# Two transformer blocks in one fp32 kernel: w_v loaded earlier into places of its own, and GpSimd, ScalarE, VectorE and TensorE work before v and k put in another order

## The reference

```python
def first_block(x, p, ...):
    h = rms_norm(x, pre_norm_gain[i])
    q, k, v, z_a, b_gate, c_gate, u, z_c = jnp.split(h @ w_in[i], N_IN_PARTS, axis=-1)
    ...
    mixed = jnp.concatenate([attn, conv_out], axis=-1) @ w_out[i]
    x = x + rms_norm(mixed, post_norm_gain[i])
    e = rms_norm(p[i] @ w_ple_proj[i], ple_norm_gain[i])
    x = x + jax.nn.sigmoid(x @ w_ple_gate[i]) * e

def gmlp_mixer(h, w_in, ln_g, ln_b, w_s, b_s, w_out):
    u, v, z = jnp.split(h @ w_in, 3, axis=-1)
    ...
    y = u * s * jax.nn.silu(z)
    return y @ w_out

def second_block(x, ...):
    y = gmlp_mixer(rms_norm_2(h, a_pre_g[i]), a_w_in[i], ..., a_w_out[i])
    h = h + rms_norm_2(y, a_post_g[i])
    kv_in = rms_norm_2(h, kv_norm_g)
    k_shared = (kv_in @ w_k).reshape(...)
    v_shared = (kv_in @ w_v).reshape(...)
    ...
    y = swa_mixer(rms_norm_2(h, b_pre_g[j]), k_shared, v_shared, b_w_in[j], b_sinks[j], b_w_out[j])
    h = h + rms_norm_2(y, b_post_g[j])
```

## Time and profile before

| what | value |
|---|---|
| median of 3 runs | 882.74 us (882.06 to 883.52) |
| the profiled execution | 882.54 us, its span 880.8 us |
| granted TensorE clock | 0.999 |
| TensorE busy | 863.5 us, 98% of the span |
| VectorE, ScalarE, GpSimd busy | 576.5, 383.7, 514.8 us |
| bytes moved by DMA | 106.84 MB |

### The profile page before, as it was taken

One profiled execution on the slowest core, in us unless ns is written; L12 is line 12 of the kernel. 1 busy time (PEld: TensorE's weight loads), 2 busy tenths in 40 slices (PEclk: granted clock), 3 DMA queues, 4 the chain that ended last, 5 costly groups with the idle time before them and its releaser, 6 DMA issues.

```text
span 880.8 us, 11945 instructions
## 1 busy us (share of the span) xinstructions
PE 863.5 (98%) x4196; PEld 718.3 (82%) x4196; DVE 576.5 (65%) x918; ACT 383.7 (44%) x828; POOL 514.8 (58%) x568
## 2 busy tenths in 40 slices
PE   8999999999998999999999999999997999999997
PEld 6888888888887788888888888888887888888875
DVE  6125648875998489676766625556995457788624
ACT  4123333433664377555112311113775446667622
POOL 7766555691249822318975048772369797566352
PEclk9999999999999999999999999999999999999999
DMA  7533222453952468994732253526951222112202
GB/s 198 165 122 97 72 78 67 142 122 73 238 194 71 138 148 176 221 234 147 175 118 85 89 169 107 133 80 163 213 173 66 72 75 93 49 48 73 72 1 95
DMA packets 83691, 106.84 MB, mean 121 GB/s; under 512 B 11953, under 2 KB 54449, under 8 KB 83634
## 3 DMA queue, kind: packets, MB, share of 16 engines
q1 hardware_dynamic: 72752, 85.12, 30.3%
q0 software_dynamic: 10880, 20.97, 14.1%
q10 hardware_dynamic: 2, 0.00, 0.0%
HBM read 103.98 MB, written 2.10 MB: 120 GB/s over the span
## 4 chain that ended last, share of the span: by engine, by line
PE 90%; POOL 5%; DVE 3%; issue 1%; ACT 0%; DMA 0%; POOLq 0%; DVEq 0%; ACTq 0%
PE bank L2186 27%; PE bank L2188 27%; PE bank L2187 27%; PE bank L2430 2%; PE bank L2458 1%; PE bank L2283 1%; DVE acc L1741 1%; POOL wlo L873 1%; PE bank L2403 1%; PE bank L2453 1%; PE bank L2452 1%; POOL ms L818 1%; DVE resid L1745 1%; POOL whi L864 1%; POOL rstd L821 1%
## 5 line engine op out<-in xcount | busy, mean ns | idle before, releaser
L873 POOL TENSOR_TENSOR wlo<-raw,whi 128x512 fp32r<-128x512 f32 x184 | 254.8, 1415 | 1.4 <-ACT whi L998 1.4
L864 POOL TENSOR_SCALAR whi<-raw 128x512 fp32r<-128x512 f32 x178 | 126.7, 750 | 174.5 <-PE bank L2188 165.7
L2186 PE MATMUL bank<-actB_hi,whi 128*128 128x512 f32 (+1 forms) x416 | 159.6, 384 | 0.6 <-POOL wlo L873 0.6
L2187 PE MATMUL bank<-actB_lo,whi 128*128 128x512 f32 (+1 forms) x416 | 158.6, 381 | 0.0
L2188 PE MATMUL bank<-actB_hi,wlo 128*128 128x512 f32 (+1 forms) x416 | 158.5, 381 | 0.0
L2186 PE MATMUL bank<-whi,actA_hi 128*128 128x512 f32 x350 | 138.1, 395 | 0.9 <-DVE actA_lo L1490 0.9
L2188 PE MATMUL bank<-whi,actA_lo 128*128 128x512 f32 x350 | 136.4, 390 | 0.0
L2187 PE MATMUL bank<-wlo,actA_hi 128*128 128x512 f32 x350 | 136.3, 389 | 0.0
L2186 PEld LDWEIGHTS bank<-actB_hi,whi 128*128 128x128 f32 x416 | 78.3, 188 | 15.6 <-issue 1.2
L2188 PEld LDWEIGHTS bank<-actB_hi,wlo 128*128 128x128 f32 x416 | 78.2, 188 | 15.1
L2187 PEld LDWEIGHTS bank<-actB_lo,whi 128*128 128x128 f32 x416 | 78.3, 188 | 14.1
(11 more groups left out here) (273 smaller groups left out, 1637.2 us busy)
## 6 DMA issues: line engine op xcount, KB each, us to landing
raw<-in_a_w_in SPq DMA_DIRECT2D x44, 512.0 KB, 4.3
raw<-in_w_in SPq DMA_DIRECT2D x32, 512.0 KB, 3.9
raw<-in_b_w_in SPq DMA_DIRECT2D x16, 512.0 KB, 3.4
raw<-in_a_w_out SPq DMA_DIRECT2D x12, 512.0 KB, 3.5
gain<-in_a_w_out POOLq DMA_DIRECT2D x9, 512.0 KB, 8.3
raw<-in_w_ple_gate SPq DMA_DIRECT2D x8, 512.0 KB, 5.1
gain<-in_a_w_in POOLq DMA_DIRECT2D x8, 512.0 KB, 7.3
raw<-in_a_w_in POOLq DMA_DIRECT2D x8, 512.0 KB, 8.1
```

The source lines that it names most:

```text
L864: pool.tensor_scalar(H, src[:, i * HALF:(i + 1) * HALF], 1.0, 1.0, ALU.mult, ALU.mult).then_inc(w_hi, 1)
L873: ins = pool.tensor_tensor(L, src[:, i * HALF:(i + 1) * HALF], H.bitcast(f32), ALU.subtract)
L2186: M(out_, whi_, xhi_, start=start, stop=False)
L2187: M(out_, whi_, xlo_, start=False, stop=False)
```

## The change

- **w_v's room.** Its two halves get a room of their own, "V": the first half in `smC` (where the spatial bias lay), the second in `gcv` (where products of z and u lay). SyncE's load waits for the last use of these places (`s4_bias`, `zu_made`) and for unit a 11's earlier load, not for room A, and stands in SyncE's program behind unit a 10's. `w_k`'s load also waits until `w_v` has landed; the first q unit's no longer follows `w_v` in room A.
- **ScalarE.** `scale_v5(0)` stands before `hi_a(9)` and `scale_v5(1)` before `hi_a(10)`. `w_k`'s scaling goes to GpSimd (8 instructions of 128x256). `hi_a(13)` is cut into its halves around `square_a(1, 1)`. `normed_n(0)` stands before `h3_out(1)`.
- **GpSimd.** All of `w_v` is split right behind its last adding DMAs, then `w_k` is scaled, then the roots a 0, a 1, h3 0 come; the later roots stand at other places in `w_k`'s split.
- **VectorE.** `lo_a(13)`, `part_gain`, `h3_in`, `add_kept(6, r)` and `rest_n` are in another order.
- **TensorE.** The turn of n 0 stands between the two blocks of A 13. In the gate, the `wt` transposes stand before the turn of x1 3.
- **Gate.** The high parts of gate unit 1 are made by ScalarE (`hi_gate`) after its squares of tile 0, not by GpSimd; the `wt` copies follow the squares of tile 1.

```diff
@@ -98,7 +98,7 @@
 ADD_A = {1: "22", 3: "22", 5: "12", 7: "12", 8: "22", 9: "22", 12: "21", 13: "21"}
 AFTER_A = {8: 5, 9: 7, 12: 8, 13: 9}
 BANKS_A = {0: 0, 3: 2, 1: 0, 2: 2, 4: 4, 5: 6, 6: 4}
-SUM_PLACES = ROOM | {"Q": (10, 11), "K": (10, 11)}
+SUM_PLACES = ROOM | {"Q": (10, 11), "K": (10, 11), "V": (10, 11)}
 
 
 def room_of(n):
@@ -108,7 +108,9 @@
         return ROOM_A[j]
     if s in ("k5", "ple"):
         return "K"
-    k = WHOLE[n] if n < UNIT_NO["v5", 0] else WHOLE[n] + (s == "v5")
+    if s == "v5":
+        return "V"
+    k = WHOLE[n]
     return "AB"[k % 2]
 
 
@@ -214,8 +216,8 @@
     o += [("S", "wo", q, r) for q in (4, 5, 6) for r in range(2)] + [("ple", t, c) for t in range(3) for c in range(2)]
     turn = lambda name, t: [("tr", name, t, j) for j in range(2)]
     o += turn("x1", 0) + [("ple", 3, c) for c in range(2)] + turn("x1", 1) + [("T", "gate", 0, 0, 0)]
-    o += turn("x1", 2) + [("T", "gate", 0, 0, 1)] + turn("x1", 3) + [("T", "gate", 0, 0, t) for t in (2, 3)]
-    o += [("wt", j) for j in range(2)]
+    o += turn("x1", 2) + [("T", "gate", 0, 0, 1)] + [("wt", j) for j in range(2)]
+    o += turn("x1", 3) + [("T", "gate", 0, 0, t) for t in (2, 3)]
     o += [("T", "gate", 0, 1, t) for t in range(2)] + [("rw", j) for j in range(2)]
     o += [("T", "gate", 0, 1, t) for t in range(2, T)]
     o += [("T", "gate", 1, 0, t) for t in range(T)] + [("T", "gate", 1, 1, t) for t in range(3)]
@@ -226,8 +228,8 @@
         for j in range(4 * half, 4 * half + 4):
             o += [("F", s, 2 * j + f) for s in ("z4", "u4") for f in range(2)]
             o += [("s4", 2 * j + f) for f in range(2)]
-        o += [("A", n, r) for n in (range(4), range(4, 14))[half] for r in range(2)]
-    o += turn("n", 0) + turn("n", 1) + [("v5", 0), ("v5", 1)]
+        o += [("A", n, r) for n in (range(4), range(4, 13))[half] for r in range(2)]
+    o += [("A", 13, 0)] + turn("n", 0) + [("A", 13, 1)] + turn("n", 1) + [("v5", 0), ("v5", 1)]
     o += [("Fa", "k5", 0)] + turn("n", 2) + [("Fa", "k5", 1)] + turn("n", 3)
     o += [("v5", 2), ("v5", 3)] + [("F", "k5", f) for f in range(2)] + [("F", "q5", f) for f in range(2)]
     for i in range(SLOTS2):
@@ -440,6 +442,7 @@
         def room_place(room, h):
 
             return {"A": raw[:, h, :], "B": raw[:, 2 + h, :], "G": gain[:, 1 + h, :], "K": tok[:, h, :],
+                    "V": gcv[:, :, :].rearrange("p a b -> p (a b)")[:, 0:D] if h else smC[:, :],
                     "Q": rest_place if h else gain[:, 0, :]}[room]
 
         def raw_of(n, h):
@@ -636,8 +639,14 @@
                     sp.wait_ge(pe_block, BLOCK["pv", 15])
                 elif (s, j) in after:
                     room_free(UNIT_NO[after[s, j]], h)
+                elif s == "v5":
+                    sp.wait_ge(s4_bias, KA)
+                    sp.wait_ge(zu_made, KA)
+                    sp.wait_ge(raw_in[10 + h], LANDED[UNIT_NO["a", 11], h])
                 elif ROOM_BEFORE[u] is not None:
                     room_free(ROOM_BEFORE[u], h)
+                if s == "k5":
+                    sp.wait_ge(raw_in[10 + h], LANDED[UNIT_NO["v5", 0], h])
                 tiles, cols = {"F": (4, 256), "T": (2, 512), "P": (1, 1024)}[kind]
                 k = k0 + tiles * h
                 src = MATRICES[name][k * P:(k + tiles) * P, c0:c0 + cols].rearrange("(k p) c -> p k c", p=P)
@@ -837,7 +846,7 @@
                 pool.wait_ge(small_in, 16 * 13)
                 for k in range(4):
                     pool.tensor_scalar(src[:, k * 256:(k + 1) * 256], src[:, k * 256:(k + 1) * 256],
-                                       bg[:, 4 * h + k:4 * h + k + 1], 1.0, ALU.mult, ALU.mult).then_inc(w_scaled, 1)
+                                       (kvg if UNITS[u][0] == "k5" else bg)[:, 4 * h + k:4 * h + k + 1], 1.0, ALU.mult, ALU.mult).then_inc(w_scaled, 1)
                 scaled[0] += 4
 
             def split_half(n):
@@ -845,11 +854,11 @@
                 u = n // 2
                 s, kind = UNITS[u][0], UNITS[u][2]
                 src, landed, value = raw_of(u, n % 2)
-                if s in ("v5", "k5"):
+                if s == "v5":
                     scaled[0] += 4
                 elif s in ("q5", "z5"):
                     scale_half(u, n % 2)
-                else:
+                elif s != "k5":
                     pool.wait_ge(landed, value)
                 if s in ("v5", "k5", "q5", "z5"):
                     pool.wait_ge(w_scaled, scaled[0])
@@ -859,7 +868,7 @@
                     pool.wait_ge(pe_block, BLOCK["s4", KA - 1])
                     pool.wait_ge(s4_bias, KA)
                     pool.wait_ge(zu_made, KA)
-                for i in range(2 if n and (s, UNITS[u][1]) != ("gate", 0) else 0):
+                for i in range(2 if n and (s, UNITS[u][1]) not in (("gate", 0), ("gate", 1)) else 0):
                     H, _ = halves_of(u, 2 * (n % 2) + i)
                     pool.tensor_scalar(H, src[:, i * HALF:(i + 1) * HALF], 1.0, 1.0,
                                        ALU.mult, ALU.mult).then_inc(w_hi, 1)
@@ -939,11 +948,12 @@
             after[at("u4", 1, 1)] = [lambda: add_a(3)]
             after[at("u4", 5, 1)] = [lambda: add_a(5)]
             after[at("u4", 7, 1)] = [lambda n=n: add_a(n) for n in (7, 8, 9, 12, 13)]
-            after[at("v5", 0, 1) - 0.25] = [lambda: root("a", 0, D), lambda: root("a", 1, D)]
-            after[at("v5", 0, 1)] = [lambda: root("h3", 0, D)]
+            after[at("v5", 0, 1)] = [lambda h=h: scale_half(UNIT_NO["k5", 0], h) for h in range(2)]
+            after[at("v5", 0, 1)] += [lambda: root("a", 0, D), lambda: root("a", 1, D), lambda: root("h3", 0, D)]
             after[at("k5", 0, 0) - 0.5] = [lambda: root("h3", 1, D)]
-            after[at("k5", 0, 1) - 0.5] = [lambda: root("a", 2, D)]
-            after[at("k5", 0, 1)] = [lambda: root("a", 3, D), lambda: root("h3", 2, D)]
+            after[at("k5", 0, 0) - 0.25] = [lambda: root("a", 2, D)]
+            after[at("k5", 0, 1) - 0.5] = [lambda: root("a", 3, D)]
+            after[at("k5", 0, 1) - 0.25] = [lambda: root("h3", 2, D)]
             after[at("q5", 0, 0) - 0.5] = [lambda: root("h3", 3, D)]
             for n in range(2 * len(UNITS)):
                 if n // 2 not in SPLIT:
@@ -1125,6 +1135,11 @@
             def square_m1(t, c):
                 act.wait_ge(c7_made, {(0, 0): 1, (0, 1): 9, (2, 1): 11, (2, 0): 13}[t // 2 * 2, c] + t % 2)
                 square("m1", t, c, out_wo(t, c))
+
+            def copied_wt():
+                for j in range(2):
+                    act.wait_ge(pe_block, BLOCK["wt", j])
+                    A(wcT[:, j * HALF:(j + 1) * HALF], psum[bank_of(("wt", j))][:, :], ACT.Copy).then_inc(wct_copied, 1)
 
             def square_e(t):
                 for c in range(2):
@@ -1170,10 +1185,11 @@
                 for j in range(2):
                     turned("x1", t, j)
                 square_e(t - 1)
+                if t == 1:
+                    hi_gate(UNIT_NO["gate", 1])
+                if t == 2:
+                    copied_wt()
             square_e(T - 1)
-            for j in range(2):
-                act.wait_ge(pe_block, BLOCK["wt", j])
-                A(wcT[:, j * HALF:(j + 1) * HALF], psum[bank_of(("wt", j))][:, :], ACT.Copy).then_inc(wct_copied, 1)
             for j in range(2):
                 act.wait_ge(pe_block, BLOCK["rw", j])
                 A(rwB[:, j * HALF:(j + 1) * HALF], psum[bank_of(("rw", j))][:, :], ACT.Copy).then_inc(rw_copied, 1)
@@ -1214,10 +1230,10 @@
                     A(hT(j)[:, :, t * P:(t + 1) * P], psum[bank_of(b)][:, :].rearrange("p (k c) -> p k c", k=4),
                       ACT.Copy).then_inc(h_copied, 1)
 
-            def hi_a(n):
+            def hi_a(n, halves=(0, 1)):
                 u = UNIT_NO["a", n]
                 act.wait_ge(pe_block, last_block(SLOT_BEFORE[u]))
-                for h in range(2):
+                for h in halves:
                     act.wait_ge(*ready_a(n, h))
                     A(halves_of(u, 2 * h, 2)[0], room_place(ROOM_A[n], h), ACT.Copy).then_inc(w7_hi, 1)
 
@@ -1373,8 +1389,8 @@
                 A(n_place(t), resid[:, t].rearrange("p (a b) -> p a b", a=2), ACT.Copy,
                   scale=rstd[:, NORMS["h3"], t:t + 1]).then_inc(tok_ready["n"], 1)
 
-            def scale_two(s, h):
-                src, landed, value = raw_of(UNIT_NO[s, 0], h)
+            def scale_v5(h):
+                src, landed, value = raw_of(UNIT_NO["v5", 0], h)
                 act.wait_ge(landed, value)
                 act.wait_ge(small_in, 16 * 13)
                 for k in range(4):
@@ -1389,24 +1405,23 @@
             hi_a(8)
             act.wait_ge(pe_block, BLOCK["A", 6, 1])
             rows_hi(actA_hi, 0, "22", hi["y4"])
+            scale_v5(0)
             hi_a(9)
             square_a(0, 0)
             square_a(1, 0)
+            scale_v5(1)
             hi_a(10)
             hi_a(11)
             square_a(2, 1)
-            scale_two("v5", 0)
             hi_a(12)
```

(20 more changed lines are left out.)

## The result

The changed kernel takes **891.11 us** (890.03 to 893.14, 4 runs), the kernel before 882.40 us on the same chip: ratio 1.0105, 95% interval 1.0093 to 1.0117. It is slower by 8.7 us by the medians and by 9.3 by the ratio, where +4.0 was forecast. The profiled execution took 890.31 us, 7.77 more than before's, its span is 888.2 us.

What follows compares the result with a forecast made beforehand. TensorE, busy 863.5 of 880.8 us, was taken as the bound. Gate -0.7, late adds +2.0, split +1.1, unit 13 +2.2 and from there to v -0.6 gave +4.0 on 882.54: 886.5 us, 8-in-10 range 879.5 to 889.0.

Steps and rivals of the forecast that it cites:

- The sign: Whole kernel: slower by over 0.2% at chance 0.62, within it 0.16, faster 0.22.
- inside units 9 to 11: TensorE's idle times there were to show the first two terms: late adds +2.0 and w_v's split +1.1.
- v's second block: Waits for rest_n(1), now behind h3_in(2) and the root a 2: 2.2 us.
- k's first: First part of k waits for w_k's last low part, behind the root h3 2 on GpSimd: 1.7 us.
- the turn of n 0: Now before unit 13's last block; 0.75 us of waiting was left for it.
- The gate: wt transposes move into the gap before the turn of x1 3: -0.7 us, ends -2.3 and 0.
- The split of w_v on GpSimd beside VectorE's low parts: GpSimd's pieces delay VectorE's low parts, so TensorE waits at unit 11: +1.1 us, ends 0 and +1.9.
- The late adds: w_v's early load delays GpSimd's adding DMAs, above all unit a 9's second half: +2.0 us, ends 0 and +2.9.
- The two terms: Units 9 to 11: w_v's early load delaying the adds, +2.0, and its split delaying VectorE's low parts, +1.1.
- Unit 13's second half: Its low part waits behind h3_in(0), root a 0 and w_k's scalings on GpSimd: +2.2 us, ends 0 and +3.4.
- rivals B: Unit 9's add is late by all of w_v's load, +2.9 in place of +2.0: 887.5 us, chance 0.10.
- D: GpSimd's chain runs early, unit 13's last block covers the turns' chain: 877.9 us, or 880 if half; chance 0.22.

Runs made afterwards that it cites:

- early: The kernel before with w_v loaded early, its scaling on ScalarE ahead of units 9 and 10 and GpSimd's split early; other orders unchanged: 887.34 us.
- hold: The whole change, but GpSimd waits with w_v's split until VectorE has made both low parts of unit a 11: 888.35 us.
- load: The kernel before with only w_v's load to its new room made early; scaling, split and orders as before: 883.26 us.
- gate: The kernel before with only the gate's part of the change: 881.05 us, ratio 0.9988.
- tail: The kernel before with only the change's orders of TensorE, VectorE and ScalarE from unit 13 on: 885.57 us.
- warm: The whole change with 40 dummy matmuls of 128 columns on TensorE where it waits ahead of unit a 10: 890.04 us.
- holdfix: hold with two VectorE steps put forward: unit 13's second low part ahead of h3_in(0), rest_n(1) ahead of h3_in(2): 890.72 us.
- tail2: tail with two VectorE steps put forward: unit 13's second low part ahead of h3_in(0), rest_n(1) ahead of h3_in(2): 883.57 us.
- roots: holdfix with GpSimd's roots a 0 and a 1 ahead of w_k's eight scalings: 889.44 us.

## Why the prediction was wrong

**The sign and the places held.** Slower was forecast at 0.62. The waits are near where they were looked for: inside units 9 to 11 (both at unit 10, where units 9 and 11 had been priced), the first block of unit 13, v's second block (forecast 2.2, measured 2.02), k's first (1.7 and 1.59), the turn of n 0 (0.75 and 0.70), none at the turns of n 1, n 2, n 3. The gate gave 0.5 in the ledger and 1.1 alone, for 0.7; x1 tile 3 got ready when it had before.

**The step that failed is "The split of w_v on GpSimd beside VectorE's low parts", +1.1.** It took the pieces one by one: 4.2 us of GpSimd's work in front of unit 11's first low part, less a slack of 2.9 and an idle time of 0.26. It had two faults.

First, the size of the collision. That each engine waits for the other was right, and early and hold show that this makes the stall. But all eight pieces, not four and a part, came before unit 10's low parts were done: GpSimd got in about two pieces for each of VectorE's instructions (eight for four), and VectorE lost 6.5 us. Unit 10, with its 2.7 us of slack, was hit, not unit 11. The late adds, +2.0 by themselves in the forecast, cost TensorE nothing at units 9 to 11 when alone (load). That term rested on a wrong reading, a slack of 0.75 us at unit 9 that counts `actA_lo` in; it is 3.0. What they did is take the slack of unit 10: VectorE's `part_gain` starts 1.5 us later than before (637.53 for 636.06) with TensorE 1.1 us ahead.

Second, **the clock was left out**. The prediction read 0.999 and priced each wait at its own length. At unit 10 TensorE stood still for 3.84 us, and the matmuls behind it ran at the 1.2 GHz level, 3.5 us more. The two terms, +3.1 in the forecast, were +8.7: the waits of 3.84 and 1.02, the 3.5, and a small rest.

**Unit 13's second half**: +0.9 for +2.2. The scalings started at 655.38 and not at 651.5, and took 8.14 us, not 3.9 (VectorE was busy beside them), so the low part was ready at 667.2, not near 664. But TensorE wanted it at 666.5 and not at 661.8, so less of the chain was left to wait for: the small size of this term is the luck of the late unit 10. hold, where TensorE was in time, shows what the chain can cost otherwise: 5.80 us of idle time, with the split held back. (The 661.8 takes no account of the gate's -0.7. And the sums of rivals B and D give 887.4 and 877.8.)

**The sum of the causes, as far as runs show them**, as differences from the kernel before on the same chip: gate -1.1; load +0.9; load and early split +6.3; the whole change +8.7. The orders from unit 13 on cost +3.3 alone (tail). The parts don't add up to the whole; that a stall hides part of the next is seen in warm and hold, where less waiting at unit 10 makes more at unit 13. How much of the change's 8.7 is the scaling of w_k on GpSimd was not measured in the change itself; only in holdfix, where it is 3.3.

## What to carry to other kernels

Idle time of GpSimd (11.24 us here) isn't free room when VectorE is full in the same stretch, as the two delayed each other: ask how much of VectorE's slack is left, and count all of the moved work against it. Take a slack up to the instruction that the waiting engine really needs; two `actA_lo` too many made 0.75 us of 3.0 here. In these runs the clock fell behind every wait of TensorE in units 9 to 13, v and k of 3.08 us or more: price such a wait at more than its length, with the matmuls behind it at half the clock. Several short waits can be cheaper than a long one, as tail2 shows against the kernel before: waits of 3.73 and 0.48 us and 883.57 us, against 5.96 us of them in six pieces and 882.13. And take a chain (norm, root, turn) to its last link before moving anything among its links: hold, holdfix and roots mostly moved the wait from one link to the next.
